# Attention on quarters and column halves of the array, with a new order of the transposes, scores and values

## What is computed

```python
# context tokens: plain attention over the 256 context keys
s = einsum('bhqd,bhkd->bhqk', q, k) * 64 ** -0.5
o = softmax(s) @ v
# latent tokens, one row of 64 queries at a time
s_win = einsum('bhqd,bhrkd->bhqrk', q_row, k_rows) * 64 ** -0.5 + bias   # 8 rows = 512 keys, bias by row and column offset
s_win = where(col_ok, s_win, -1e30)                                      # 16 of 64 columns are seen
s_ctx = einsum('bhqd,bhld->bhql', q_row, k_ctx) * 64 ** -0.5             # 256 cached context keys
p = softmax(concatenate([s_win, s_ctx]))
o = p[..., :512] @ v_rows + p[..., 512:] @ v_ctx
```

## Time and profile before

| | us |
|---|---|
| median of 3 runs | 2512.56 (2512.36 to 2512.92) |
| the profiled execution, own time | 2510.91 |
| its span, first to last instruction | 2509.1 |
| mean granted clock of TensorE | 0.983 |
| TensorE busy (matmul) | 2382.1 (95%) |
| VectorE busy | 1296.3 (52%) |
| ScalarE busy | 725.6 (29%) |
| GpSimd busy | 657.8 (26%) |

### The profile page before, as it was taken

One profiled execution on the slowest core, in us unless ns is written; L12 is line 12 of the kernel. 1 busy time (PEld: TensorE's weight loads), 2 busy tenths in 40 slices (PEclk: granted clock), 3 DMA queues, 4 the chain that ended last, 5 costly groups with the idle time before them and its releaser, 6 DMA issues.

```text
span 2509.1 us, 50765 instructions
## 1 busy us (share of the span) xinstructions
PE 2382.1 (95%) x21658; PEld 1964.0 (78%) x21658; DVE 1296.3 (52%) x2077; ACT 725.6 (29%) x1189; POOL 657.8 (26%) x283
## 2 busy tenths in 40 slices
PE   5899999999999998889999998999999999999997
PEld 4777878788888887888745687888888888888886
DVE  4575657527568667895543323634333433443344
ACT  5273644634455553333300001201100110011002
POOL 2022020111211111222000244434344444444341
PEclk9999999999999999999989998999999999999999
DMA  6313111022266786676423310111111111111112
GB/s 281 109 35 106 55 60 62 28 95 76 93 193 193 202 230 191 196 204 183 154 75 115 119 35 26 34 34 43 35 42 34 43 34 43 34 42 37 40 34 93
DMA packets 224561, 234.53 MB, mean 93 GB/s; under 512 B 143922, under 2 KB 178866, under 8 KB 222898
## 3 DMA queue, kind: packets, MB, share of 16 engines
q1 hardware_dynamic: 199090, 229.55, 28.4%
q10 hardware_dynamic: 25344, 3.15, 0.8%
HBM read 173.80 MB, written 57.02 MB: 92 GB/s over the span
## 4 chain that ended last, share of the span: by engine, by line
PE 81%; DVE 8%; issue 3%; ACT 2%; DMA 2%; SPq 1%; ACTq 1%; POOL 1%; DVEq 0%; POOLq 0%
PE PS L878 20%; PE PS L879 20%; PE PS L880 20%; PE PS L1354 6%; PE PS L1022 3%; PE PS L994 2%; DVE buffer L2081 2%; PE PS L1008 1%; DVE buffer L2080 1%; PE PS L996 1%; DMA buffer<-in_w_ada_first 1%; ACTq L1729 1%; PE PS L1074 1%; PE PS L1164 1%; PE PS L1326 1%
## 5 line engine op out<-in xcount | busy, mean ns | idle before, releaser
L878 PE MATMUL PS<-buffer,buffer 128*128 128x512 f32 (+1 forms) x2784 | 997.5, 358 | 10.2 <-DVE buffer L1976 3.4
L879 PE MATMUL PS<-buffer,buffer 128*128 128x512 f32 (+1 forms) x2784 | 987.8, 355 | 1.7 <-issue 1.7
L880 PE MATMUL PS<-buffer,buffer 128*128 128x512 f32 (+1 forms) x2784 | 987.8, 355 | 0.0
L878 PEld LDWEIGHTS PS<-buffer,buffer 128*128 128x128 f32 x2784 | 525.6, 189 | 97.3 <-issue 17.0
L880 PEld LDWEIGHTS PS<-buffer,buffer 128*128 128x128 f32 x2784 | 525.6, 189 | 78.8 <-issue 2.1
L879 PEld LDWEIGHTS PS<-buffer,buffer 128*128 128x128 f32 x2784 | 525.9, 189 | 75.2 <-issue 1.0
L2366 POOL TENSOR_TENSOR buffer<-buffer,buffer 128x1024 fp32r<-128x1024 f32 x76 | 184.0, 2421 | 816.8 <-PE PS L880 510.4
L2309 DVE SCALAR_TENSOR_TENSOR buffer<-PS,buffer,buffer 128x512 f32<-128x512 f32 (+1 forms) x264 | 158.5, 655 | 151.4 <-PE PS L880 151.4
L2367 POOL TENSOR_TENSOR buffer<-buffer,buffer 128x1024 fp32r<-128x1024 f32 x76 | 194.1, 2554 | 6.0
L2285 DVE TENSOR_SCALAR buffer<-buffer,buffer 128x1281 f32<-128x1281 f32 x22 | 34.8, 1582 | 286.6 <-ACT buffer L1810 286.6
L1810 ACT ACTIVATE buffer<-PS 128x512 f32<-128x512 f32 (+1 forms) x66 | 30.0, 529 | 504.3 <-PE PS L880 504.3
(11 more groups left out here) (228 smaller groups left out, 2796.9 us busy)
## 6 DMA issues: line engine op xcount, KB each, us to landing
buffer<-in_w_up SPq DMA_DIRECT2D x44, 512.0 KB, 3.3
buffer<-in_w_in SPq DMA_DIRECT2D x42, 512.0 KB, 5.2
ops_kept<-buffer SPq DMA_DIRECT2D x40, 512.0 KB, 4.6
buffer<-ops_kept SPq DMA_DIRECT2D x80, 256.0 KB, 3.4
buffer<-in_w_ada SPq DMA_DIRECT2D x32, 512.0 KB, 6.3
buffer<-rkv_kept SPq DMA_DIRECT2D x120, 128.0 KB, 3.3
buffer<-in_w_down SPq DMA_DIRECT2D x22, 512.0 KB, 3.3
buffer<-in_x SPq DMA_DIRECT2D x20, 512.0 KB, 7.6
```

The source lines that it names most:

```text
L878: mm(out, w_hi, x_hi, start=start, stop=False)
L879: mm(out, w_hi, x_lo, start=False, stop=False)
L880: return mm(out, w_lo, x_hi, start=False, stop=stop)
```

## The change

**TensorE, scores.** The queries lie densely in `qT` (features on partitions), and each head is multiplied on its own quarter of the array: 64 rows (features) by 64 columns (queries). An even unit uses the quarters on the diagonal, an odd unit the other two, so its heads come out swapped. Units are taken in pairs: `scores(u)` issues the window scores of u, the context scores of u+1, the window scores of u+1, then, after a wait on its own context scores of u+1 (`side_scored`), the context scores of u. Window scores lie in bank 0 (even units) and banks 1 and 2 in turn (odd units); context scores of a pair share bank 3 or 4. That makes five score banks.

**TensorE, values.** Each head's values are a product of 128 rows by 64 columns (one column half of the array) with 64 moving columns, in bank 7: 24 passes per latent unit in place of 12, each with half the moving columns.

**TensorE, order.** Step t is: transposes of t-2, then (t even) the scores of t+2 and t+3, then the values of t-4. Window transposes go to bank 5, context transposes to bank 6. All waits inside the transposes are as before.

**VectorE.** A `tensor_tensor_reduce` adds window scores and bias, scaled by -1/8, and takes the row minimum; a second one does the context scores (with a tile of zeros) and carries the minimum on. They replace L1957, L1963 and ScalarE's L1559. VectorE copies the four window transposes (512 columns, before: 256), and one 128x64 block of values in place of two 64x64. Step t is: reciprocal of t-1, transposed copy of t-3, output copy of t-4, scores of t+1.

**ScalarE.** Copies the two context transposes (256 columns, before: 512 for latent units); step t is: that copy of t-3, normalisation of t-1, exponential of t, with scale -1.

**The rest.** A second bias table with the heads swapped, made by two DMAs on SyncE's queue ahead of those of `vodd`; register arithmetic ahead of some waits (`hold`) on TensorE and VectorE; the memset of `qbd` and ScalarE's second query copy go.

Cut to its core (removed lines of the loops stand in the kernel above; here "..." marks them):

```diff
-    put("win_ok", ok)
+    put("win_ok", ok / SCALE)
...
+        zeros = const("zero").to_broadcast([P, CTX])
...
-        qbd = s2(NU, P)
+        qT = s2(T)
...
+        bias_swapped = s2(NDR, 64)
+        s2.at = max(s2.at, EARLY_END)
...
-        rowstat = s2(3, 3)
+        rowstat = s2(3, 4)
...
+        def win_bank(u):
+            return 0 if u % 2 == 0 else 1 + u // 2 % 2
+        def ctx_scores(u):
+            s = u // 2 % 2
+            if u < 4 and u % 2:
+                return PS[:, 1 + s, 0:CTX]
+            return PS[:, 3 + s, u % 2 * CTX:(u % 2 + 1) * CTX]
...
+                sp.wait_ge(proj_out_d, i * PROJ_D + 5)
+                for hh in range(2):
+                    sp.dma_start(one_head(bias_swapped, hh), one_head(bias, 1 - hh)).then_inc(vodd_in, 16)
...
+                def hold(sem, base, count):
+                    pe.reg_add(awaited, base, count)
+                    pe.wait_ge(consts_in, 32)
+                    pe.wait_ge(sem, awaited)
+                def scores(u):
+                    if u >= 4:
+                        hold(ctx_out, units, u - 1)
+                    def one(v, part):
+                        for h in range(2):
+                            f, o = slice(64 * h, 64 * h + 64), slice(64 * (h ^ v % 2), 64 * (h ^ v % 2) + 64)
+                            if part == 0:
+                                r0, _ = unit_window(v)
+                                ins = mm(PS[o, win_bank(v), :], qT[f, v * 64:v * 64 + 64], kT[f, CTX + GRID * r0:CTX + GRID * r0 + 512],
+                                         start=True, stop=True)
+                            else:
+                                keys = kcT if v >= 4 else kT[:, 0:CTX]
+                                ins = mm(ctx_scores(v)[o], qT[f, v * 64:v * 64 + 64], keys[f], start=True, stop=True)
+                        return ins
+                    if u >= 4:
+                        one(u, 0)
+                    ins = one(u + 1, 1)
+                    if u >= 4:
+                        ins.then_inc(side_scored, 1)
+                        one(u + 1, 0)
+                        hold(side_scored, pairs, (u - 2) // 2)
+                    one(u, 1).then_inc(scored, 1)
+                def values(u):
+                    nb = 2 if u < 4 else 6
+                    pe.wait_ge(pt_out_a, i * NU + u + 1)
+                    if u >= 4:
+                        pe.wait_ge(pt_out_d, i * ROWS + (u - 3))
+                    if u >= 1:
+                        pe.wait_ge(o_out, i * 2 * NU + 2 * u)
+                    if u == 4:
+                        pe.wait_ge(vodd_in, i * 64 + 64)
+                    for b, (src, at) in enumerate(unit_keys(u)):
+                        for h in range(2):
+                            q = 64 * (h ^ u % 2)
+                            ins = mm(PS[64 * h:64 * h + 64, 7, 0:64], src[:, at, 64 * h:64 * h + 64],
+                                     pT[u % 2][:, b, q:q + 64], start=(b == 0), stop=(b == nb - 1))
+                    ins.then_inc(o_done, 1)
+                def transposes(u):
+                    pe.wait_ge(p_ready, i * NU + u + 1)
+                    if u >= 1:
+                        pe.wait_ge(pt_out_a, i * NU + u)
+                    if u >= 5:
+                        pe.wait_ge(pt_out_d, i * ROWS + (u - 4))
+                    for b in range(0 if u < 4 else 4):
+                        pe.transpose(PS[:, 5, b * P:(b + 1) * P], scr[:, u % 3, b * P:(b + 1) * P], ident)
+                    for b in range(2):
+                        ins = pe.transpose(PS[:, 6, b * P:(b + 1) * P], scr[:, u % 3, 512 + b * P:512 + (b + 1) * P], ident)
+                    ins.then_inc(pt_done, 1)
+                pe.reg_mul(units, i, PROJ_D)
+                hold(proj_out_d, units, PROJ_D)
+                pe.reg_mul(units, i, NU)
+                pe.reg_mul(pairs, i, ROWS // 2)
+                scores(0)
+                for t in range(NU + 4):
                     if 2 <= t < NU + 2:
...
+                        transposes(t - 2)
+                    if t % 2 == 0 and t + 2 < NU:
+                        scores(t + 2)
+                    if t >= 4:
+                        values(t - 4)
                 pe.wait_ge(o_out, i * 2 * NU + 2 * NU)
...
+            with ExitStack() as counts:
+                units, pairs, awaited = (counts.enter_context(pe.register(n)) for n in ("units", "pairs", "awaited"))
+                with pe.Fori(0, NP) as i:
+                    attention(i)
...
-                    src = PS[:, g, 0:n].rearrange("p (u t) -> p u t", t=64)
-                    dst = qbd[:, t0 // 64:(t0 + n) // 64, :]
...
+                    act.activation(qT[:, t0:t0 + n], PS[:, g, 0:n], ACT.Copy).then_inc(proj_out_a, 1)
...
                 for t in range(NU + 3):
...
+                    if t >= 3:
+                        u = t - 3
+                        at = 0 if u < 4 else 4
+                        act.wait_ge(pt_done, i * NU + u + 1)
+                        if u >= 2:
+                            act.wait_ge(o_done, i * NU + u)
+                        act.activation(pT[u % 2][:, at:at + 2, :].rearrange("p b n -> p (b n)"), PS[:, 6, 0:2 * P], ACT.Copy) \
+                            .then_inc(pt_out_a, 1)
                     if 1 <= t <= NU:
                         u = t - 1
                         lo = 512 if u < 4 else 0
                         act.wait_ge(recip_ready, i * NU + u + 1)
                         act.activation(scr[:, u % 3, lo:768], scr[:, u % 3, lo:768], ACT.Copy,
                                        scale=rowstat[:, u % 3, 2:3]).then_inc(p_ready, 1)
...
                     if t < NU:
                         u = t
                         lo = 512 if u < 4 else 0
...
+                        act.wait_ge(ctx_out, i * NU + u + 1)
+                        act.activation(scr[:, u % 3, lo:768], scr[:, u % 3, lo:768], ACT.Exp, scale=-1.0,
                                        bias=rowstat[:, u % 3, 0:1], accum_out=rowstat[:, u % 3, 1:2]).then_inc(exp_done, 1)
-            act.wait_ge(pool_steps, 4)
-            with A.loop(0, NP, 3) as i:
+            with act.Fori(0, NP) as i:
...
                 dve.wait_ge(proj_out_d, i * PROJ_D + PROJ_D)
...
+                def hold(sem, base, count):
+                    dve.reg_add(awaited, base, count)
+                    dve.wait_ge(consts_in, 32)
+                    dve.wait_ge(sem, awaited)
+                def scores_out(u):
+                    if u >= 3:
+                        dve.wait_ge(pt_done, i * NU + (u - 2))
+                    if u == 5:
+                        dve.wait_ge(vodd_in, i * 64 + 64)
+                    hold(scored, pairs, u // 2 + 1)
+                    least = 3.0e38
+                    if u >= 4:
+                        _, b0 = unit_window(u)
+                        least = rowstat[:, u % 3, 3:4]
+                        dve.tensor_tensor_reduce(scr[:, u % 3, 0:512], PS[:, win_bank(u), :],
+                                                 (bias, bias_swapped)[u % 2][:, b0 // 64:b0 // 64 + 8, :].rearrange("p d c -> p (d c)"),
+                                                 -SCALE, 3.0e38, ALU.add, ALU.min, least).then_inc(win_out, 1)
+                        hold(win_out, rows, u - 3)
+                    dve.tensor_tensor_reduce(scr[:, u % 3, 512:768], ctx_scores(u), zeros, -SCALE, least, ALU.add, ALU.min,
+                                             rowstat[:, u % 3, 0:1]).then_inc(ctx_out, 1)
+                dve.reg_mul(pairs, i, NU // 2)
+                dve.reg_mul(rows, i, ROWS)
+                scores_out(0)
+                for t in range(NU + 4):
                     if 1 <= t <= NU:
                         u = t - 1
                         dve.wait_ge(exp_done, i * NU + u + 1)
                         dve.reciprocal(rowstat[:, u % 3, 2:3], rowstat[:, u % 3, 1:2]).then_inc(recip_ready, 1)
...
+                    if 7 <= t < NU + 3:
                         u = t - 3
+                        dve.wait_ge(pt_done, i * NU + u + 1)
+                        dve.wait_ge(o_done, i * NU + u)
+                        dve.tensor_copy(pT[u % 2][:, 0:4, :].rearrange("p b n -> p (b n)"), PS[:, 5, :]).then_inc(pt_out_d, 1)
+                    if t >= 4:
+                        u = t - 4
                         dve.wait_ge(o_done, i * NU + u + 2)
...
+                        dst = ybT[:, bass.ds(i, 1), u * 64:(u + 1) * 64].rearrange("p a t -> p (a t)")
+                        dve.tensor_copy(dst, PS[:, 7, 0:64]).then_inc(o_out, 2)
+                    if t + 1 < NU:
+                        scores_out(t + 1)
...
-            pool.wait_ge(h_done, 3 * KB)
-            G.link(pool.memset(qbd[:, :, :], 0.0))
```

More of the change, by code:

```diff
@@ L100, in constants @@
     put("head_in", hin)
+    put("zero", np.zeros((P, 1)))
     put("sum_parts", p[:, None] % 32 == np.arange(2)[None, :])
@@ L1945, in attention @@
                 dve.wait_ge(proj_out_d, i * PROJ_D + PROJ_D)
-                for t in range(NU + 3):
```

(9 more changed lines are left out.)

92 lines of the change are left out of this document (2 added, 90 removed).

## The result

The changed kernel takes **2706.72 us** (median of 4 runs, 2695.88 to 2711.36) against 2512.46 of the kernel before (4 runs, 2511.92 to 2512.92): ratio 1.0759, 95% interval 1.0734 to 1.0784. Forecast were 2602, at most 2670. The sign was right, the size was not: +194 in place of +90. The profiled execution took 2709.95, its span 2708.1.

The account below looks back on a forecast made before the run. TensorE alone bound the old kernel; the new order makes TensorE and VectorE alternate, lengthening each pair's loop from 65.4 to 87.9 us, +90 over four pairs. 2510.9 + 90 = 2601, plus the median's 1.65 gives 2602 us; range 2570 to 2670.

Parts of the forecast that it names:

- the ring: Steps 7 to 18 of a pair's loop: TensorE and VectorE take turns, mean step 5.09 us against 3.29 before.
- Both waits: Transposes of t-2 wait for VectorE's same-step copy of t-3; output copy of t-4 waits for same-step values behind transposes and scores.
- That sum: Pieces of a step in turn, from transposed copy to reciprocal: 4.36 us odd, 5.82 even, mean 5.09.
- VectorE's part: Output copy 0.24, reductions 0.79 and 0.53, reciprocal 0.20, 512-column copy 0.68, then TensorE's release 0.14 us.
- the odd step: Step without new scores: copy, transposes, values, output copy, two reductions and reciprocal in turn, 4.36 us.
- the even one: Step with a pair's scores ahead of the values: 1.46 us more than an odd step, 5.82 us.
- TensorE's clock falls: Rival: same alternation, but TensorE idles each step and drops to 1.2 GHz; 2727 us, 2664 for half the time; chance 0.16.
- the eleven steady steps: Steps 8 to 18 of a pair's loop: five of 5.82 us and six of 4.36 us.
- The head: Start of a pair's loop, from first scores to the end of VectorE's step 7: 21.0 us.
- The tail: End of a pair's loop: steps 19 to 21 without reductions, then two values with their copies, 11.6 us.
- Do the array's parts overlap?: Quarters and column halves run at once: a pair's scores 1.46 us, values 0.67; rival of parts in turn, 2638 or 2677, chance 0.13.
- The no-ring rival: Copy and values met a step ahead, so VectorE's 2.44 us per unit is the period: 2458 us, chance 0.03.

Follow-up runs that it names:

- e4: Changed kernel with TensorE's step as values, scores, transposes and a fourth score slot in place of three: 2494.25 us, ratio 0.9903 to 0.9942 against the kernel before.
- e8: Kernel before with its old products, put in the change's order on TensorE, VectorE and ScalarE: 2736.16 us, ratio 1.0874 to 1.0957.
- e6: Changed kernel plus two unread 512-column products on TensorE behind each output copy of steps 4 to 21: 2654.08 us, ratio 1.0552 to 1.0627 against before.
- e1: Changed kernel plus three unread 384-column products on TensorE behind the values in odd steps from 7: 2661.34 us, ratio 1.0566 to 1.0610 against before.
- e9: Kernel before with each values product split into two halves of 64 moving columns: 2627.23 us, ratio 1.0418 to 1.0465.
- e12: Changed kernel, order kept, with TensorE's loop over the four pairs written out: 2681.76 us, ratio 1.0632 to 1.0691 against the kernel before.
- e10: Four-slot kernel e4 with TensorE's loop over the four pairs written out: 2456.45 us, ratio 0.9759 to 0.9795 against the kernel before.

## Why the prediction failed in size

- **What bounds the kernel, and the ring:** right. Both waits, their order and the alternation stand in the trace, and e4 and e8 show that the order makes them. At a clock of 1.00 the mean step is (4.16 + 6.01) / 2 = 5.09, the forecast's number to the last digit; that it agrees so closely is luck.
- **That sum has errors that cancel.** The pair's scores take 1.85 (156.56 to 158.41 in e6), not 1.46: the context scores of unit u start 1.27 behind the first product. Ahead of them stands the wait on `side_scored`, which I gave no price; that it makes the difference is not shown. The values take 0.85 (187.54 to 188.39 in e1), not 0.67, and the output copy follows their stream by 0.22 (188.61 in e1), not 0.37. VectorE's part, from output copy to first transpose, is 2.29 in place of 0.24 + 1.32 + 0.20 + 0.68 + 0.14 = 2.58: the second reduction starts 0.84 behind the first and the reciprocal 0.41 behind that. So the odd step was forecast 0.20 too long and the even one 0.19 too short.
- **The step that failed: the clock, taken as 1.00.** I had it as a rival, "TensorE's clock falls", at 0.16, with 2664 for half the time low and 2727 for all of it. The clock was low in about 60% of the loops (0.68 to 0.73 granted over whole loops, between 0.50 and 1.00), for which the rival's price is 75. The loops measured 86 over the forecast, 21.6 each. Of these, 14.6 are the eleven steady steps, and e6, with the clock held, shows them to be the clock's. The head added 4.4: output copy 3 starts 22.4 to 26.1 behind the first scores (309.28 less 286.28 in the second pair), mean 23.8, where the forecast had 21.0 - 1.32 - 0.24 = 19.4. The tail added 2.6 (15.5 from output copy 14 to the last, forecast 12.9). The clock is low there too (0.88 and 0.79 in the two parts of the second head, 0.68 in the tail), but it is not all of it: in e6's second loop, whose head was granted 1.00, output copy 3 still starts 21.7 behind the first scores, with the fillers in between. How head and tail divide is not shown. That 2706.72 lies between 2664 and 2727 is in part chance, since it holds the 23 us of the next point, which the rival did not have. "No row shows 40%" was true, and the nearest rows (0.50 and 0.67 where TensorE was nearly idle) should have pulled the likeliest case down, not only the range. The Trainium skill, TensorE: Matmul & The Clock Gate, Part 1, says that the clock is set by how busy the array has recently been; e1 and e6 agree, since added work alone brought it back.
- **A term that was missing: the stretches between the loops.** I priced TensorE's new passes only where they run. They also lengthen the turn to which TensorE returns: +6.3, +7.0 and +9.5 = 23 us. e9 shows it in the old kernel, and e12 takes it off.
- **Do the array's parts overlap?** Yes, as forecast from L1036. In e6 eight window passes, four of them into bank 0 from two row halves, are issued and followed by the context scores within 1.27; one by one the eight would take 8 x 0.43 = 3.4. The Trainium skill, TensorEngine Tiling (Array Packing), Gotcha 1: PSUM Pressure, would have them take turns in one bank; the row speaks against it here too.
- **`hold`, bound 0 to 0.1 each:** e10's even step is 3.11 and e4's 3.28, so two of them cost 0.17, near the upper bound, where TensorE is nearly the bound. Whether they cost anything in the ring is not shown.
- **The no-ring rival**, 2458 at VectorE's 2.44 per unit: e10 comes out there, but by luck and by another bound. Its two steps take 5.26 (2.63 per unit, not 2.44), TensorE is busy for 18.2 of 20 us and VectorE for 15.2, and it needs a fourth slot and a loop written out, which the change has not.

## What to carry to other kernels

Before shortening products, draw for each engine in which step a value is made and in which it is used; where a reordering puts both into the same step on two engines, their work adds up, and a cut to the products cannot pay for it. When the same ring leaves the matrix engine idle every few us, price its clock too: useless work that brings the clock back can be cheaper than idling. And count the instructions in a turn of a hardware loop: cutting products into smaller ones can cost several us at every return.

## What was not expected of the hardware

- Filling the idle stretch of the ring made the kernel 1.7% faster (e1) and 1.9% (e6), without a result being used.
- A pass of 64 moving columns over the whole array costs as much as one of 128: 24 passes from 163.30 to 165.93 in e9 are 0.110 each, against 1.34 / 12 = 0.112 before. I had taken half. On column halves the same 24 passes take 0.85, 0.035 each: what makes them cheap is the half weights, or that two run at once (no run separates these); fewer moving columns alone do not.
- A turn of TensorE's loop with 208 more passes, all engines and data otherwise the same (e9), makes the return 3.7 us dearer (4.88 against 1.16 of idle time) and holds the first products at 1.2 GHz for some 4.6 us. From the second turn on, the instruction queue moves 9 packets per turn in place of none.
